# Attention in groups of two stages: twelve transposes in three PSUM banks, scores of two stages, values of two in one bank

## What is computed

```python
def nsa_mixer(h, ...):            # 16 heads of 64 in 4 key groups
    q, kc, vc, ks, vs, kw, vw, gates = split(h @ w_in)
    k_cmp, v_cmp = compress(kc, ...), compress(vc, ...)      # 15 blocks of 32 tokens
    p_c = masked_softmax(q @ k_cmp * scale + bias_c, mask_c) # compressed branch
    o_cmp = p_c @ v_cmp
    ...                            # with 256 tokens every block is selected
    o_sel = masked_softmax(q @ ks * scale + bias) @ vs       # selected branch
    o_win = masked_softmax(q @ kw * scale + bias) @ vw       # window branch
    return (g[0] * o_cmp + g[1] * o_sel + g[2] * o_win) @ w_out

def fox_mixer(h, ...):
    q, k, v, f_logit = split(h @ w_in)
    cum = cumsum(log_sigmoid(f_logit + b_f))
    p = masked_softmax(q @ k * scale + cum[query] - cum[key])
    return (p @ v) @ w_out
```

## Time and profile before

| | us |
|---|---|
| median of 3 runs | 1020.52 |
| lowest and highest | 1020.27 and 1021.84 |
| the profiled execution | 1019.52 |
| its span, first to last instruction | 1017.70 |

### The profile page before, as it was taken

How to read it: one execution, slowest core, us unless ns; L and a number is a source line. 1 busy time by engine, 2 the same in 40 slices (tenths; PEclk the granted TensorE clock), 3 DMA queues, 4 the chain that set the end, 5 groups by cost and what they waited for, 6 DMA issues and landing times.

```text
span 1017.7 us, 13823 instructions
## 1 busy us (share of the span) xinstructions
PE 1006.0 (99%) x5707; PEld 850.6 (84%) x5707; DVE 638.0 (63%) x761; ACT 519.5 (51%) x712; POOL 118.8 (12%) x213
## 2 busy tenths in 40 slices
PE   8999999999999999999999999999999999999997
PEld 7888888897767898888889888888888689888886
DVE  5656565747686765655576655557568776555654
ACT  5544445644564555444465444445456665454442
POOL 1000000213263300000030000001103320000000
PEclk9999999999999999999999999999999999999999
DMA  9767778367403365566825565692485345565651
GB/s 267 251 203 251 234 258 294 99 187 235 138 2 125 124 207 182 191 197 215 292 83 191 183 205 174 200 312 102 138 282 176 111 144 175 198 192 181 206 177 73
DMA packets 138422, 189.55 MB, mean 186 GB/s; under 512 B 7442, under 2 KB 120439, under 8 KB 138360
## 3 DMA queue, kind: packets, MB, share of 16 engines
q1 hardware_dynamic: 133734, 172.83, 52.5%
q0 software_dynamic: 4480, 15.77, 4.7%
q10 hardware_dynamic: 146, 0.07, 0.0%
HBM read 185.99 MB, written 1.09 MB: 184 GB/s over the span
## 4 chain that ended last, share of the span: by engine, by line
PE 96%; DVE 1%; DMA 1%; ACT 1%; POOL 0%; issue 0%; DVEq 0%; ACTq 0%; POOLq 0%
PE ps L1201 93%; PE ps L1618 2%; PE ps L1422 1%; DMA kvN<-kvN 1%; DMA cst<-in_consts 0%; DVE work L955 0%; DVE late L974 0%; POOL work L468 0%; ACT work L663 0%; PE ps L1496 0%; DVE normed L857 0%; POOL ms L435 0%; ACT normed L719 0%; DVE wlo L808 0%; ACT whi L556 0%
## 5 line engine op out<-in xcount | busy, mean ns | idle before, releaser
L800 DVE TENSOR_TENSOR wlo<-raw,whi 128x2048 fp32r<-128x2048 f32 x140 | 321.1, 2293 | 122.9 <-ACT whi L548 122.9
L1201 PE MATMUL ps<-xhl,whi 128*128 128x512 f32 (+1 forms) x1664 | 387.5, 376 | 0.0
L1201 PEld LDWEIGHTS ps<-xhl,whi 128*128 128x128 f32 x1664 | 287.5, 189 | 50.7 <-issue 2.8
L548 ACT ACTIVATE whi<-raw 128x2048 fp32r<-128x2048 f32 x145 | 276.8, 1909 | 29.1 <-DMA raw<-in_ffn_w_up 8.3
L1201 PEld LDWEIGHTS ps<-xhl,wlo 128*128 128x128 f32 x1536 | 207.9, 190 | 13.8
L1201 PE MATMUL ps<-xhl,wlo 128*128 128x256 f32 x1536 | 213.1, 282 | 0.0
L1201 PE MATMUL ps<-whi,hhi 128*128 128x512 f32 x320 | 124.9, 390 | 0.0
L1201 PE MATMUL ps<-wlo,hhi 128*128 128x512 f32 x320 | 124.9, 390 | 0.0
L1201 PE MATMUL ps<-whi,hlo 128*128 128x512 f32 x320 | 124.5, 389 | 0.0
L1201 PE MATMUL ps<-whi,xhl 128*128 128x512 f32 (+1 forms) x464 | 115.0, 372 | 0.0
L1201 PEld LDWEIGHTS ps<-whi,xhl 128*128 128x128 f32 x464 | 81.2, 189 | 16.1 <-issue 2.6
(11 more groups left out here) (175 smaller groups left out, 811.9 us busy)
## 6 DMA issues: line engine op xcount, KB each, us to landing
raw<-in_ffn_w_down SPq DMA_DIRECT2D x44, 1024.0 KB, 5.0
raw<-in_ffn_w_up SPq DMA_DIRECT2D x40, 1024.0 KB, 5.3
raw<-in_ffn_w_gate SPq DMA_DIRECT2D x37, 1024.0 KB, 5.3
raw<-in_fox_w_in SPq DMA_DIRECT2D x9, 1024.0 KB, 5.4
raw<-in_nsa_w_in SPq DMA_DIRECT2D x7, 1024.0 KB, 5.5
big<-in_nsa_cmp_w POOLq DMA_DIRECT2D x8, 512.0 KB, 6.6
raw<-in_nsa_w_out SPq DMA_DIRECT2D x4, 1024.0 KB, 5.9
raw<-in_fox_w_out SPq DMA_DIRECT2D x4, 1024.0 KB, 5.1
```

Of the source, the lines that this page charges most:

```text
L548: nc.scalar.activation(whi[:, u % RING, :], raw_of(u), ACT.Copy).then_inc(w_hi, 1)
L800: nc.vector.tensor_tensor(wlo[:, u % RING, :], raw_of(u), whi[:, u % RING, :].bitcast(F32), ALU.subtract).then_inc(w_lo, 1)
L1201: return nc.tensor.matmul(out_, l, r, start=start, stop=stop)
```

## The change

Stages are handled two by two. `turn(g)` on TensorE transposes stages 2g and 2g+1 in one run of twelve, 512 columns to each of the banks GB, GB+1 and GB+2 (bank 6, the former OB), with a wait and a signal for each bank. VectorE copies each bank with one 512-wide copy (`turned_out`). In a step j TensorE does the transposes of group j-2, the scores of stages 2j and 2j+1, then the heads of both stages of group j-2. The values of two stages go to one bank, HB = 7: for NSA that is one pair (256 columns), for FoX two pairs (512). ScalarE's and VectorE's splits work on a whole group (`group_hi`, `group_lo`). There is one value bank and one `probT` in place of two, so `heads` of a group waits for `group_lo` of the one before, and the copies of a group wait for the heads of the one before.

The compressed part moves between groups and from bank MB to OB: `compress_hidden(1)` now follows scores(0), `second_compressed` follows the heads of group 0, `turn_scores(1)` those of group 1, and `compressed_T(1)`, which replaces both `later_T`, those of group 3. The third bank of groups 0, 1, 2 and 4 waits for the compressed part to leave OB. VectorE's `compressed_logits(1)` goes ahead of the copies of group 2, `compressed_max(1)` behind logits(8), `compressed_probs(1)` behind logits(11). ScalarE's `scores_out(1)` goes from step 3 to behind exps(5).

The diff, without the pure renaming of banks:

```diff
@@ scalar, attend
-                for i in range(EARLY_STAGES[kind], N + LAG + 2):
-                    if i >= LAG + 2 and (i - LAG - 1) % per == 0:
-                        heads_hi((i - LAG - 1) // per - 1)
-                    if i < N:
-                        exps(kind, n0 + i)
+                def group_hi(g):
+                    act.wait_ge(heads_mm, n0 + 2 * g + 2)
+                    k, m = 2 * g // per, 2 // per
+                    nc.scalar.activation(xhi[:, k:k + m, :], ps[:, HB, 0:m * S].rearrange("p (k n) -> p k n", k=m), ACT.Copy).then_inc(ohi_ready, m)
+                for i in range(EARLY_STAGES[kind], N):
+                    if i > 4 and i % 2 == 1:
+                        group_hi(i // 2 - 2)
+                    exps(kind, n0 + i)
                     if i in after_exps:
                         after_exps[i]()
-                    if i in (N, N + 2):
-                        hi(out_unit + (i - N) // 2)
+                hi(out_unit)
+                group_hi(N // 2 - 2)
+                hi(out_unit + 1)
+                group_hi(N // 2 - 1)
...
-                    attend(kind, u0 + nproj + 2, {3: lambda: scores_out(1), 6: lambda: compressed_exp(1)} if kind == "nsa" else {})
+                    attend(kind, u0 + nproj + 2, {5: lambda: scores_out(1), 8: lambda: compressed_exp(1)} if kind == "nsa" else {})
@@ vector, logits
                 if n >= PB:
-                    dve.wait_ge(probT_mm, n - PB + 1)
+                    dve.wait_ge(probT_mm, 3 * (n // 2 - 2) + 2 + n % 2)
@@ vector, attend
+                def turned_out(g):
+                    for b in range(3):
+                        dve.wait_ge(probT_mm, 3 * g + b + 1)
+                        if g:
+                            dve.wait_ge(heads_mm, 2 * g)
+                        nc.vector.tensor_copy(probT_buf[:, 512 * b:512 * b + 512], ps[:, GB + b, :]).then_inc(probT_ready, 1)
+                def group_lo(g):
+                    k, m = 2 * g // per, 2 // per
+                    dve.wait_ge(ohi_ready, p0 + k + m)
+                    nc.vector.tensor_tensor(xlo[:, k:k + m, :], ps[:, HB, 0:m * S]..., ALU.subtract).then_inc(olo_ready, m)
+                G_ = N // 2
+                for i in range(EARLY_STAGES[kind], 4):
+                    logits(kind, n0 + i)
                     if i in after_logits:
                         after_logits[i]()
-                    if i == N:
+                    if i:
                         factors(kind, n0 + i - 1)
+                for j in range(2, G_ + 2):
+                    if j in before_turned:
+                        before_turned[j]()
+                    turned_out(n0 // 2 + j - 2)
+                    if j >= 3:
+                        group_lo(j - 3)
+                    if j <= G_:
+                        factors(kind, n0 + 2 * j - 1)
+                    for i in (2 * j, 2 * j + 1):
+                        if j < G_:
+                            logits(kind, n0 + i)
+                        if i in after_logits:
+                            after_logits[i]()
+                    if j < G_:
+                        factors(kind, n0 + 2 * j)
+                    elif j == G_:
                         lo(out_unit)
+                lo(out_unit + 1)
+                group_lo(G_ - 1)
@@ tensor, attend
+                def turn(g, ready={}):
+                    for b in range(3):
+                        pe.wait_ge(prob_ready, 2 * g + min(b, 1) + 1)
+                        if g:
+                            pe.wait_ge(probT_ready, 3 * g - 2 + b)
+                        if b in ready:
+                            ready[b]()
+                        for c in range(4 * b, 4 * b + 4):
+                            a, k = c // 3, c % 3
+                            last = nc.tensor.transpose(ps[:, GB + b, (c % 4) * P:(c % 4 + 1) * P],
+                                                       prob[(2 * g + a // 2) % PB][:, a % 2, k * P:(k + 1) * P], ident)
+                        last.then_inc(probT_mm, 1)
                 def heads(n):
                     b = n % 2
-                    pe.wait_ge(probT_ready, n + 1)
+                    pe.wait_ge(probT_ready, 3 * (n // 2) + 2 + b)
                     pair = (n - n0) // per
-                    if pair >= 2:
-                        pe.wait_ge(olo_ready, p0 + pair - 1)
-                    bank = OB + pair % 2
+                    if n > n0 and b == 0:
+                        pe.wait_ge(olo_ready, p0 + pair)
+                    c0 = (pair % (2 // per)) * S
...
+                for i in range(4):
+                    scores(n0 + i)
                     if i < EARLY_STAGES[kind]:
                         project(nproj - EARLY_STAGES[kind] + i)
                     if i in after_scores:
                         after_scores[i]()
+                G_ = N // 2
+                for j in range(2, G_ + 2):
+                    turn(n0 // 2 + j - 2, free.get(j, {}))
+                    if j < G_:
+                        for i in (2 * j, 2 * j + 1):
+                            scores(n0 + i)
+                    elif j == G_:
+                        pe.wait_ge(logits_ready, n0 + N)
+                        out_rows(0, 0)
+                    else:
+                        out_opening(0)
+                    for i in (2 * j - 4, 2 * j - 3):
+                        heads(n0 + i)
+                    if j == G_:
+                        out_rows(0, 1)
+                    elif j > G_:
+                        out_opening(1)
+                    elif j in after_heads:
+                        after_heads[j]()
...
+                    attend(kind, {0: lambda: compress_hidden(1), 1: last_projection, 2: lambda: compress_out(1), 3: lambda: compressed_T(0)},
+                           {2: second_compressed, 3: lambda: turn_scores(1), 5: lambda: compressed_T(1)}, out_rows, out_opening,
+                           {2: {0: lambda: pe.wait_ge(proj_ready, pr0 + nproj), 2: lambda: pe.wait_ge(probcT_ready, 1)},
+                            3: {2: lambda: pe.wait_ge(sc_copied, 2)}, 4: {2: lambda: pe.wait_ge(sc_step, 6)},
+                            6: {2: lambda: pe.wait_ge(probcT_ready, 2)}})
```

More of the change, by code:

```diff
@@ L728, in scores_out @@
                             act.wait_ge(sc_mm, 1)
-                        nc.scalar.activation(scoresT, ps[:, MB if r else YB + 2, 0:S], ACT.Copy).then_inc(sc_copied, 1)
+                        nc.scalar.activation(scoresT, ps[:, OB if r else YB + 2, 0:S], ACT.Copy).then_inc(sc_copied, 1)
                     def compressed_exp(r):
@@ L997, in attend @@
-                    if i >= LAG + 2 and (i - LAG - 1) % per == 0:
-                        heads_lo((i - LAG - 1) // per - 1)
+                for j in range(2, G_ + 2):
[14 more added lines that the diff above has]
+                    elif j == G_:
+                        lo(out_unit)
@@ L1566, in compress_out, with attend @@
                 last.then_inc(cmp_mm, 1)
[L1568 removed]
+            def attend(kind, after_scores, after_heads, out_rows, out_opening, free, project=None, nproj=0):
                 n0, p0, N = STAGE0[kind], PAIR0[kind], STAGES[kind]
@@ L1642, in heads @@
                     for a in range(2):
-                        mm(ps[side(a), bank, 0:S], values(n, a, 0), probT[:, b, a, 0:S], kind == "fox", False)
+                        mm(ps[side(a), HB, c0:c0 + S], values(n, a, 0), probT[:, b, a, 0:S], kind == "fox", False)
                     for a in range(2):
-                        last = mm(ps[side(a), bank, P:S], values(n, a, 1), probT[:, b, a, S:SCORES], False, final)
+                        last = mm(ps[side(a), HB, c0 + P:c0 + S], values(n, a, 1), probT[:, b, a, S:SCORES], False, final)
                     last.then_inc(heads_mm, 1)
-                for i in range(N + LAG + 1):
-                    if i < N:
-                        scores(n0 + i)
+                for i in range(4):
+                    scores(n0 + i)
                     if i < EARLY_STAGES[kind]:
@@ L1711, in compressed_scores @@
                             c0 = 32 * (pair - 4 * r)
-                            last = mm(ps[c0:c0 + 32, MB if r else YB + 2, 0:S], kcmp[:, 2 * pair // G, :, :].rearrange("p a c -> p (a c)"),
+                            last = mm(ps[c0:c0 + 32, OB if r else YB + 2, 0:S], kcmp[:, 2 * pair // G, :, :].rearrange("p a c -> p (a c)"),
                                       qT[:, pair, :], True, True)
@@ L1718, in turn_scores @@
                         for t in range(TT):
-                            last = nc.tensor.transpose(ps[:, MB if r else YB + 2, S + t * P:S + (t + 1) * P], scoresT[:, t * P:(t + 1) * P], ident)
+                            last = nc.tensor.transpose(ps[:, OB if r else YB + 2, S + t * P:S + (t + 1) * P], scoresT[:, t * P:(t + 1) * P], ident)
                         last.then_inc(sc_mm, 1)
                     def last_projection():
-                        compress_hidden(1)
                         project(9, lambda: compress_fold(1))
```

101 lines of the change are left out of this document (21 added, 80 removed).

## The result

The changed kernel takes 1022.11 us (median of 17 runs, 1020.17 to 1023.20) against 1020.38 us for the kernel before (17 runs beside them, 1019.28 to 1021.84): a ratio of 1.0014, with an interval of 1.0008 to 1.0021. It is slower by 1.7 us, 0.8 to 2.1, which is just inside the 0.2% that the prediction called no difference. The forecast was 1022.7 us.

The account below looks back on a forecast made before the run. TensorE, busy 99% of the span, was taken as the bound. NSA +2.05 and FoX -0.1, with inner waits at 0.05, gave +2.15 us on 1020.52, so 1022.7 us; eight-in-ten range 1020.0 to 1025.1.

Parts of the forecast that it names:

- The loop: Steady groups: VectorE waits 0.92 us for fresh exponentials, copies queued behind; loop over VectorE and ScalarE 5.4 in NSA, 5.7 in FoX.
- The rival in which the loop does not bind: Exponentials are ready when VectorE asks; with exponentials of half the length -2.3 us, 1018.2 us; chance 0.10.
- The waits: Added waits of TensorE summed over each stretch: +5.85 us in NSA, +1.7 in FoX.
- GpSimd: First NSA group: TensorE idles 1.5 us until GpSimd has scaled stage 1, which the second bank needs.
- the bank of the compressed scores: Second NSA group: third bank OB waits for scores_out(1), queued behind exps(5) on ScalarE; 1.4 us idle.
- compressed probabilities: Third to sixth NSA group: compressed_T(1) on TensorE waits 1.9 us for VectorE's compressed probabilities, heads done.
- ahead of heads: TensorE waits some 0.5 us ahead of heads for group_lo.
- The term of 0.05 for each inner wait: Waits inside a run of transposes, two per group, 24 in all, taken at 0.05 us each.
- the rival that a wait costs what a switch does: Waits at a block's head cost, not shape: 0.15 us per inner wait, some four per group; +4.5, 1025.0 us; chance 0.10.
- the switches: Shape switches on TensorE, 23 fewer in NSA, 11 in FoX, at 0.15 or 0.20 us: -3.8 (walk's count) and -1.75.
- two walks: Four engine queues stepped through in old and new order; old walk within 0.6 us of NSA's trace, so differences were used.
- The rival on the compressed part: The compressed part fits wholly into VectorE's waits for exponentials: +0.3 us, 1020.8 us, no difference; chance 0.26.

Follow-up runs that it names:

- the undisturbed traces: Single further profiled execution of the unedited changed kernel, no clock fall in NSA or FoX: 1020.36 us, NSA 82.51, FoX 38.88, before at 1020.76 beside it.
- the last experiment but one: Changed kernel with row products again between the two heads of the last two groups of NSA and FoX: single execution 1023.26 us, before at 1020.76.
- the repeat: Changed kernel run again without edit, 12 runs: 1021.97 us, ratio 1.0013 to the kernel before (1020.47) beside it.

## Why the prediction came out as it did

**What held.** The direction, the size within 0.6 us, and the range. The likeliest case lay just above the border of 0.2%, the result lies just below it.

- The bound, and where the gain would go. TensorE works 3.5 us less and the kernel gets no faster. The loop was forecast at 5.4 to 5.45 with 0.92 us of standing still; it is 5.44 with 0.82. Moving that wait made the group 5.15, so it was the loop and not something beside it. The rival in which the loop does not bind falls. Three copies of 512 columns take 1.78 from start to start (310.93 to 312.71), so the 0.60 for each held.
- The waits, one by one: GpSimd 1.27 (forecast 1.5), the bank of the compressed scores 1.3 (1.4), compressed probabilities 1.70 (1.9), start 0.65 (0.6), ahead of heads 0.33 and 0.37 (0.5). In FoX, TensorE's timeline shows 0.46, 1.43 and 0.40 (0.6, 1.6, 0.7). All are where they were forecast; all but the one at the start are 0.1 to 0.3 smaller.

```profile
796.35 1.09 PE L1631 MATMUL ps<-cst,normed 128*128 128x128 f32 x8 [0.46 <-POOL normed L469]
...
800.38 1.52 PE L1213 MATMUL ps<-late,big 128*64 128x256 f32 x16 [1.43 <-DVE xhl L983]
...
813.64 1.52 PE L1213 MATMUL ps<-late,big 128*64 128x256 f32 x16 [0.40 <-DVE xhl L983]
```

- That a wait which is met costs nothing. Twelve transposes with three waits and three signals take 1.46 from start to start, 12 x 0.11 + 0.15. The term of 0.05 for each inner wait is 0, and the rival that a wait costs what a switch does falls. The 26 ns which the Trainium skill (TensorE: Matmul & The Clock Gate, The cost: per-tile semaphore tail) gives for a signal do not show in TensorE's starts either; the page counts them at the end of a run, which these rows cannot show.

**What was mis-sized.** The sum was +2.15 us, and the undisturbed traces give +1.3: NSA +1.6 for +2.05 and FoX −0.35 for −0.1, beside 0.2 for inner waits that cost nothing. The windows of the two stretches split it. Each line gives the stretch, its length and TensorE's busy time; the rest of the length is TensorE's idle time. First the kernel before, NSA and FoX:

```profile
258.28:339.16 80.88, 79.05 (x578) 55.45 (x578) 57.49 (x202) 47.94 (x159) 36.35 (x70) 1.00 0.21 67
785.90:825.15 39.25, 38.31 (x243) 28.46 (x243) 27.56 (x73) 22.38 (x62) 12.99 (x31) 1.00 0.33 108
```

Then the changed kernel, undisturbed:

```profile
257.78:340.29 82.51, 75.98 (x577) 56.65 (x577) 57.74 (x209) 47.42 (x159) 36.54 (x70) 1.00 0.21 66
787.08:825.96 38.88, 36.59 (x243) 28.95 (x243) 27.57 (x73) 22.05 (x58) 13.25 (x32) 1.00 0.34 109
```

The idle time rose by 4.70 us in NSA and 1.35 in FoX, 6.05 together; the waits were forecast at 5.85 and 1.7, 7.55 together. The busy time fell by 3.07 and 1.72, 4.8 together; the switches were forecast at 3.8 and 1.75, 5.55 together. So the term that was mis-sized is the waits: 1.5 us too large, as the single waits above are, whose differences add up to 1.4. The switches gave back 0.8 less than forecast, which made up for half of it. (Idle time is counted from the modelled end of a product, some 0.1 us behind the point where the next one could have started. There are five waits more than before, so that up to 0.5 us moves from the work to the waits: +6.5 and −5.2. Both terms stay below the forecast.)

The waits came from the difference of two walks. The walk over the order of before fell 0.6 us short of its trace in NSA, and I took it that the walk over the new order would fall short alike. It did not: NSA from scores(0) to the close is 70.25 in the undisturbed trace (forecast 70.6 by the difference), and the walk by itself came within 0.3 of that. Why the two walks erred differently stays open. The second side of a border, which the last experiment but one puts at 0.01 to 0.04 a switch above the 0.15, is no explanation: with 34 switches saved it would have made TensorE's work fall by more than was forecast, and it fell by less.

That the total came within 0.5 us of the forecast rise (+1.7 for +2.15) is in part luck: the sum was 0.85 too high, and the falls of the clock, which it does not contain, put some of that back.

**What was missed.** That a wait of TensorE can cost more than its length. The prediction counts 1.5 us of idle time in the first group as slack that partly comes back, and says nothing of the clock. In the executions where the clock falls behind it, 1.3 us more are lost (1.2 to 1.5 in three traces), as much as all else that the change costs. Counted over the profiled executions: with the first gap of 1.27 left open there were seven (the changed kernel three times, and the kernels with later factors, earlier probabilities, earlier copy, and switches put back), and the clock fell in four. With the gap filled there were four, and it fell in none of them at that place; in one of these it fell behind the wait of 2.35 that had grown in the next group. In before, the longest idle stretch at this place is 0.59 and there was no fall.

Four of seven against none of four is few, and does not show by itself that the wait sets off the fall. The mean granted clock of all executions points the same way: 0.9982 for the changed kernel (29 executions), 0.9988 with the gap filled (12), 0.9989 for before (60). A fall of 3.41 us to one half takes 0.0017 off the mean of an execution, so by this estimate it falls in about one execution in three of the changed kernel. There is an exception: the kernel with earlier probabilities, gap open, has 0.9988 too. Nor is it the length of a wait alone: the same traces hold waits of 1.70 us (ahead of the turned compressed probabilities, in eight of them) and of 1.43 us (in FoX, in nine), and the clock fell behind none of these.

The Trainium skill (TensorE: Matmul & The Clock Gate, A second HAM failure mode: psum-queue depth-cycling) tells of a kernel whose short idle stretches between groups of products made the clock go down and up again. The rows here agree in that a wait of 1.27 us sufficed, in four of seven executions.

**The rival on the compressed part** was half true. It is not free, as the earlier probabilities and the earlier copy show (0.7 us of the total and 1.2 us of NSA); but its cost lies in the two steps that decide when it comes out, and each can be had back by one number.

**What stays open.** How much the falls of the clock cost on average. The traces say 1.3 us in somewhat over half of the executions, 0.7 us in the mean; the mean clock says one in three, 0.4 to 0.5 us. With the +1.3 of the undisturbed kernel that is 1.7 to 2.0, where 1.7 was measured. But the kernel with the gap filled, which has no falls in two traces, was not faster in its totals than the repeat (1022.07 and 1021.97), and its long times do not go with a low mean clock (eight with 0.999 lie between 1020.62 and 1022.74). The start of scores(0) scatters by over 2 us from execution to execution, and in both of its traces it was late (259.1 and 259.6); the part behind FoX scatters as well, between 192.5 and 194.0. For neither have I a cause that I could show. Nor do the rows say why the clock falls in one execution and not in another: the idle stretches ahead of it are the same to 0.01 us. The reason for the +0.35 at the start (`compress_hidden(1)` ahead of scores(1)) was forecast and seen, and not tried by itself.

## What to carry to other kernels

Merging the steps of one engine saves its switches, but it also merges the requests to the others: ask of every engine in the loop which fresh result it now waits for, and what could have run in the meantime but is queued behind. Here four such places, among them one reciprocal ahead of a ready copy and one copy behind the wrong exponentials, turned a gain of 0.3% into a loss of 0.1%. And when two walks are subtracted, do not count on their errors cancelling: what one walk falls short by against its own trace need not be missing from the other.

## What the runs showed of the chip that was not expected

- After a wait of 1.27 us on TensorE, with another of 0.5 shortly before, the granted clock went from 1.00 to 0.50 in four of seven executions, every time for 3.41 us. In two of them the sixteen score products behind it took 2.86 in place of 1.51 us; in the two where it fell earlier, the eight transposes took 1.8 in place of 1.0 and the scores 2.4. It fell once behind a wait of 2.35, and never behind the waits of 1.70 and 1.43 further on.
- Changing between 128x512 products and 128x64 tiles costs 0.16 to 0.19 us for each change, and a pair of changes shows as 0.09 ahead of the block, 0.15 in it, and 0.11 behind.
